# State space chunks begun ahead of the preceding chunk's state, convolution steps spread over the projections, queries projected ahead of gates

## The reference, cut to what matters

```python
# layer of the first network (conv branch): 31 taps, depthwise, 256 wide
u = conv_in * sigmoid(conv_gate)
y = conv_b + sum(u_padded[:, k:k+T] * conv_w[k] for k in range(31))
y = silu(layernorm(y) * ln_g + ln_b) * silu(out_gate)
# differential attention: k, q rotated; two softmaxes of 48-wide heads, subtracted,
# normed, times silu(gate)

def rwkv7_step(S, inp):
    r_t, w_t, k_t, v_t, kk_t, a_t = inp
    sa = jnp.einsum("bhvk,bhk->bhv", S, -kk_t)
    S = (S * w_t[:, :, None, :]
         + jnp.einsum("bhv,bhk->bhvk", sa, kk_t * a_t)
         + jnp.einsum("bhv,bhk->bhvk", v_t, k_t))
    y = jnp.einsum("bhvk,bhk->bhv", S, r_t)
    return S, y
```

## Time and profile before

| | us |
|---|---|
| median of 3 runs | 3750.78 |
| lowest, highest | 3741.96, 3754.45 |
| the profiled execution | 3754.05 |
| its span in the trace | 3752.3 |
| TensorE busy in the span | 3362.2 (90%) |
| late stage of layer 0, projections to first scores | about 285 to 513 |
| late stage of layer 1, same | about 900 to 1064 |
| chunks of the matrix recurrence | about 1818 to 2154 |

### The profile page before, as it was taken

How to read it: one execution, slowest core, us unless ns; L and a number is a source line. 1 busy time by engine, 2 the same in 40 slices (tenths; PEclk the granted TensorE clock), 3 DMA queues, 4 the chain that set the end, 5 groups by cost and what they waited for, 6 DMA issues and landing times.

```text
span 3752.3 us, 40013 instructions
## 1 busy us (share of the span) xinstructions
PE 3362.2 (90%) x16212; PEld 2633.0 (70%) x16212; DVE 1673.2 (45%) x2537; ACT 1226.9 (33%) x2071; POOL 737.2 (20%) x547
## 2 busy tenths in 40 slices
PE   3999687799988999986699889999999999989998
PEld 1878565587766788864577757887788876567886
DVE  2153556324864634353533345343634342445344
ACT  2242155334254322322221233223322233733222
POOL 1203111431413100163211130000100053240000
PEclk6999898899998999998776789999999999999999
DMA  4303110121102232322000012323232321012322
GB/s 182 109 36 113 68 37 15 56 90 43 61 11 75 80 98 97 96 76 72 1 1 1 1 51 85 101 91 100 79 96 99 93 89 62 1 51 93 104 92 77
DMA packets 77575, 260.95 MB, mean 70 GB/s; under 512 B 8400, under 2 KB 9552, under 8 KB 76240
## 3 DMA queue, kind: packets, MB, share of 16 engines
q1 hardware_dynamic: 76528, 253.67, 20.5%
q0 software_dynamic: 864, 4.72, 0.4%
HBM read 256.26 MB, written 2.10 MB: 69 GB/s over the span
## 4 chain that ended last, share of the span: by engine, by line
PE 82%; DVE 10%; ACT 4%; POOL 2%; issue 1%; DMA 1%; SPq 0%; POOLq 0%; ACTq 0%; DVEq 0%
PE banks L343 81%; DVE area L1659 2%; PE banks L352 1%; DMA x_lat<-in_xt 1%; POOL area L400 1%; DVE area L852 1%; DVE area L551 1%; DVE small L1713 1%; POOL w_lo L334 1%; DVE x_lat L554 0%; DVE area L472 0%; DVE area L2459 0%; DVE area L461 0%; ACT area L417 0%; ACT w_hi L324 0%
## 5 line engine op out<-in xcount | busy, mean ns | idle before, releaser
L343 PE MATMUL banks<-area,w_hi 128*128 128x512 f32 (+4 forms) x5896 | 1777.9, 385 | 60.6 <-POOL w_lo L334 27.1
L343 PEld LDWEIGHTS banks<-area,w_hi 128*128 128x128 f32 (+2 forms) x5896 | 1085.9, 189 | 324.5 <-issue 52.6
L343 PE MATMUL banks<-area,w_lo 128*128 128x512 f32 (+3 forms) x2948 | 1125.3, 383 | 0.0
L343 PE MATMUL banks<-area,area 128*128 128x64 f32 (+11 forms) x3888 | 590.1, 356 | 73.6 <-DVE area L2503 12.1
L343 PEld LDWEIGHTS banks<-area,w_lo 128*128 128x128 f32 (+2 forms) x2948 | 558.5, 189 | 119.6
L343 PE MATMUL banks<-area,w_late 128*128 128x512 f32 (+2 forms) x2316 | 576.4, 398 | 39.3 <-ACT area L507 21.1
L343 PEld LDWEIGHTS banks<-area,area 128*128 128x128 f32 (+4 forms) x3888 | 464.4, 203 | 194.7 <-issue 101.1
L343 PEld LDWEIGHTS banks<-area,w_late 128*128 128x128 f32 (+1 forms) x2316 | 435.0, 190 | 153.6 <-ACT area L507 24.4
L324 ACT ACTIVATE w_hi<-w_raw 128x1024 fp32r<-128x1024 f32 (+2 forms) x361 | 349.5, 971 | 560.5 <-PE banks L343 432.4
L400 POOL TENSOR_TENSOR area<-area,area 128x512 f32<-128x512 f32 (+1 forms) x114 | 152.5, 1340 | 1536.8 <-ACT area L385 1534.2
L334 POOL TENSOR_TENSOR w_lo<-w_raw,w_hi 128x1024 fp32r<-128x1024 f32 (+1 forms) x133 | 302.9, 2280 | 512.2 <-ACT w_hi L324 512.2
(11 more groups left out here) (235 smaller groups left out, 2329.4 us busy)
## 6 DMA issues: line engine op xcount, KB each, us to landing
w_raw<-in_l_ffn_w_in SPq DMA_DIRECT2D x176, 512.0 KB, 3.3
w_raw<-in_l_ffn_w_out SPq DMA_DIRECT2D x128, 384.0 KB, 3.1
w_raw<-in_w_in SPq DMA_DIRECT2D x66, 512.0 KB, 3.5
w_raw<-in_w_mod SPq DMA_DIRECT2D x32, 512.0 KB, 5.0
w_raw<-in_w_qkv SPq DMA_DIRECT2D x24, 512.0 KB, 3.3
w_raw<-in_l_w_in SPq DMA_DIRECT2D x22, 512.0 KB, 3.3
w_raw<-in_w_out SPq DMA_DIRECT2D x32, 320.0 KB, 2.9
area<-in_w_mod SPq DMA_DIRECT2D x8, 1024.0 KB, 14.2
```

Source lines behind the costliest of these rows:

```text
L343: return e.matmul(out, lhsT, rhs, start=first, stop=stop, skip_group_check=True)
```

## The change

In `LateStage` the queries are projected ahead of the gates, on all engines and in the order of the weights, and the layer norm's steps move to the groups of the gates. The 62 taps are dealt out by a table: 10 after the convolution's inputs (ahead of modulation third 1), 6 behind it, then 4 per rotation of the keys, 2 (layer 0) or 4 (layer 1) per copy of the values, then the copy of modulation third 2, then 4 or 2 per rotation of the queries, and the rest. In `EvenMixer` a chunk is cut into begin (masked B, xs), keys (tok, masked K), levels and state; begin of chunk c+1 is issued between levels and state of chunk c, and keys of c+1 after the state part of c. For this `xt_m` and `m_rb_t` have two buffers, in space from a smaller `levels` table (8 masks instead of 14) and from two dead tiles.

```diff
-LATE_GROUPS = (8, 9, 2, 3, 7, 6)
+LATE_GROUPS = (8, 9, 2, 3, 6, 7)
 class LateStage:
-            TAPS_EACH = 4
-                self.ln_at = {"mean": 1, "sum": (4, 6), "square": (2, 5), "root": (5, 7)} if two else {
-                    "mean": 0, "sum": (2,), "square": (1,), "root": (3,)}
+                self.taps_at = (10, 6, 4, 2, 4) if two else (10, 6, 4, 4, 2)
+                self.ln_at = {"mean": 1, "square": (1, 3), "sum": (2, 4), "root": (2, 4), "silu": 6} if two else {
+                    "mean": 0, "square": (0,), "sum": (1,), "root": (1,), "silu": 2}
 # pe
                 self.mod_pe(q, e, 2)
-                self.g_of.pe(q, e)
                 self.rope_pe(q, e, self.q_of, "q")
+                gates = [(m, s) for m, s, *_ in self.g_of.each()]
+                self.g_of.pe(q, e, lambda q, e, m, s: self.ln_pe(q, e, gates.index((m, s))))
                 self.mod_pe(q, e, 3)
 # dve
                 self.conv_dve(q, e)
+                taps = self.taps(q, e)
+                for _ in range(self.taps_at[0]):
+                    next(taps, None)
                 self.mod_dve(q, e, 1)
-                self.rope_dve(q, e, self.k_of, "k", some_taps)
-                self.v_of.dve(q, e, some_taps)
+                for _ in range(self.taps_at[1]):
+                    next(taps, None)
+                some = lambda n: lambda i: [next(taps, None) for _ in range(n)]
+                self.rope_dve(q, e, self.k_of, "k", some(self.taps_at[2]))
+                self.v_of.dve(q, e, some(self.taps_at[3]))
+                self.mod_dve(q, e, 2)
+                self.rope_dve(q, e, self.q_of, "q", some(self.taps_at[4]))
                 for _ in taps:
                     pass
-                self.mod_dve(q, e, 2)
-                self.rope_dve(q, e, self.q_of, "q", lambda i: self.ln_dve(q, e, i))
+                self.ln_dve(q, e)
                 self.mod_dve(q, e, 3)
 class EvenMixer:
 # pe
+                self.begin_pe(q, e, 0)
+                self.keys_pe(q, e, 0)
                 for c in range(NCH):
-                    self.chunk_pe(q, e, c, beside)
+                    self.levels_pe(q, e, c, beside)
+                    if c + 1 < NCH:
+                        self.begin_pe(q, e, c + 1)
+                    self.state_pe(q, e, c, beside)
+                    if c + 1 < NCH:
+                        self.keys_pe(q, e, c + 1)
 # dve
+                    self.levels_dve(q, e, c, beside)
+                    self.mid_dve(q, e, c)
+                    next(beside, None)
+                    if c + 1 < NCH:
+                        self.begin_dve(q, e, c + 1)
+                    self.state_dve(q, e, c)
+                    if c + 1 < NCH:
+                        self.keys_dve(q, e, c + 1)
+            def begin_dve(self, q, e, c):
                 if c:
-                    q.wait_ge(*at(self.tag, "made", "y", c - 1))
+                    for g in range(2):
+                        q.wait_ge(*at(self.tag, "off", c - 1, 6, g))
+                        q.wait_ge(*at(self.tag, "made", "t1", c - 1, 6, g))
+                if c >= 2:
+                    q.wait_ge(*at(self.tag, "made", "y", c - 2))
...
+            def keys_dve(self, q, e, c):
+                if c:
+                    q.wait_ge(*at(self.tag, "made", "y", c - 1))
+                for half in range(2):
+                    self.masked_dve(q, e, c, "K", half)
```

More of the change, by code:

```diff
@@ L1447, in rope_act @@
                         q.wait_ge(*at("turned", t))
-                for g, (m, s, c0, c1, u, bank) in enumerate(project.each()):
+                for m, s, c0, c1, u, bank in project.each():
                     round_weights(q, e, project.pieces[m])
@@ L1601, in act @@
                 self.v_of.act(q, e)
-                for m, s, c0, c1, u, bank in self.g_of.each():
+                self.rope_act(q, e, self.q_of, "q", self.qd)
+                for g, (m, s, c0, c1, u, bank) in enumerate(self.g_of.each()):
                     round_weights(q, e, self.g_of.pieces[m])
@@ L1958, in __init__ @@
                 self.tot = place.take(4, 3 * NCH)
-                self.levels = place.take(14, P)
+                self.levels = place.take(8, P)
                 chunk_at = place.at
@@ L2008, in __init__, with books_masked @@
                     self.books("var heads", p), self.books("gate", p)
+            def books_masked(self, c, kind):
+                if kind == "K":
+                    for i in range(3):
+                        self.books("tok", c, i)
+                for half in range(2):
+                    for odd in range(2):
+                        self.books("masked", c, kind, half, odd)
+                if kind == "B":
+                    for g in range(2):
+                        self.books("xs", c, g)
             def books(self, *key):
@@ L2125, in masked_pe, with begin_pe @@
                     self.made(t, *key)
-            def chunk_pe(self, q, e, c, beside):
+            def begin_pe(self, q, e, c):
                 cs = slice(c * CH, (c + 1) * CH)
-                if c == 0:
-                    for who in ("dve", "act", "pool"):
-                        q.wait_ge(*at("fence", who, "even chunks"))
-                for i in range(3):
-                    src, dst = self.tok(i, c)
-                    self.bank_free(q, "tok", c, i)
-                    for p in range(4):
-                        t = turned(e, self.bank("tok", c, i)[:, p * P:(p + 1) * P], src(p))
-                    self.made(t, "tok", c, i)
                 for half in range(2):
@@ L2146, in chunk_pe, with keys_pe, levels_pe @@
                     self.made(t, "xs", c, g)
+            def keys_pe(self, q, e, c):
+                for i in range(3):
+                    src, dst = self.tok(i, c)
+                    self.bank_free(q, "tok", c, i)
+                    for p in range(4):
+                        t = turned(e, self.bank("tok", c, i)[:, p * P:(p + 1) * P], src(p))
+                    self.made(t, "tok", c, i)
                 for half in range(2):
                     self.masked_pe(q, e, c, "K", self.k_t, half)
+            def levels_pe(self, q, e, c, beside):
                 for n_l in range(1, 7):
```

125 lines of the change are left out of this document (66 added, 59 removed).

## The result

The changed kernel takes 3659.34 us, the median of four runs (3654.36 to 3670.15), against 3750.59 us for the kernel before (3741.96 to 3754.45): a ratio of 0.9764, with a 95% interval of 0.9735 to 0.9793. The forecast was 3652, the range 3630 to 3690.

A forecast was written before the change was run, and what follows sets the result against it. TensorE was taken as the bound (82% of the chain of waits), through its waits and half clock. Terms 31.6 + 12.2 + 14.5 + 13.5 + 27.4 = 99.2 us off 3754.05, less 3.3 for the median, gave 3652 us; range 3630 to 3690.

The forecast's parts named there:

- Layer 0: Late stage of layer 0: 33.4 us wait for VectorE's rows' copy becomes 5.6, stage end gains 4.8, 1.0 lost: 31.6 us gained.
- "I take 0" for the ten taps ahead of third 1: Layer 0: taps moved into VectorE's silences were taken to cost nothing; without that cover the price is 3 us.
- A wait for L334 over 2 us: Sign that the forecast is wrong: TensorE newly waiting over 2 us for L334, a low half of weights from GpSimd.
- Layer 1: Late stage of layer 1: 3.6 us tap wait goes, half clock returns 2.5, the end gains about 6.1: 12.2 us.
- Chunks, idle time: Chunks: inverse wait gone in three of four (9.1 us), scaled-state wait filled (net 3.6), chunk 0 earlier (1.8): 14.5 us.
- Chunks, clock of the levels: Chunks, ahead of the levels: no wait after y, so 11.2 us at half clock become full, three times: 13.5 us.
- Chunks, clock of the state part: Chunks, rhs to y: two of three state parts taken at full clock, 27.4 us; 0 and 41 kept as ends.
- the first rival: State part of the chunks: three small waits keep its clock from ever holding, term 0; 3679 us, chance 0.30.
- the fourth: Late stages: GpSimd, slowed beside taps, starves TensorE of weights, kernel slower; 3769 us, chance 0.03 together with a null result.
- the second: Chunks: even the levels stay at half clock for their first 13 us, only idle time goes; 3693 us, chance 0.06.
- third: Chunks: all three state parts hold full clock and the levels' waits shrink too; 3638 us or less, chance 0.13.
- fifth: Layer 0: TensorE still stands at modulation third 2 for another reason, layer 0 gives only 4; 3680 us, chance 0.03.

## Why the prediction was right, and where it was not

The time is 7 us above the forecast, inside the range. That it is so near is in part luck: the largest term in doubt, 27.4 us, came to nothing, and some 16 us that the working did not have (behind layer 1, in the levels and in the waits of the chunks) made up for more than half of it. Step by step, on the profiled execution (83.9 us against 99.2):

- **Layer 0, 31.6 us: 27.1 measured.** The wait went from 33.4 to 6.8 us where 5.6 was worked out, 26.6 us instead of 27.8. The end of the stage and all the rest, by difference, gave 4.5, where the working had 3.8 (4.8 less 1.0). Two terms were not in it: 2.4 us for the low half, and 1.6 us by which this execution was already late ahead of the stage (VectorE's last product there at 304.18, before at 302.60). "I take 0" for the ten taps ahead of third 1 was the step that failed: I had asked what VectorE's silence covers and not what GpSimd does in it. A wait for L334 over 2 us was among the signs of being wrong, and it came, at one place.
- **Layer 1, 12.2 us: 12.5 measured** (39.6 less 27.1). The tap wait is gone, and ahead of the scores 0.94 us are left. (The working took 0.2 us off for what stays there, though it named 0.7.)
- **Behind layer 1** lie 6.8 us that I had not counted (46.4 less 39.6). The run with the late stages alone has 7.1 us there too (50.5 less 43.4), so it comes with that half of the change; which part of it is attention at another clock no run tells.
- **Chunks, idle time, 14.5 us: 16.7 measured** (20.8 less 1.8 and 2.3). The wait of about 0.95 us for a bank ahead of rhs did not come: rhs takes the banks of the first masked products, and VectorE had read these by 1825.39 (L2531), just as TensorE came to rhs. By the busy times of the two traces the idle time fell from 29.3 to 12.8 us, which agrees.
- **Chunks, clock of the levels, 13.5 us: some 20.8, by difference** (37.5 less 16.7). The return just behind y came as foretold. The rest of these 20.8 us is not the first half of the levels alone. In chunks 0 to 2 rhs now runs longer at 2.4 GHz before the clock falls: it took some 7.3 us instead of 8.67 in chunk 0 and some 6.4 instead of 9.93 in chunk 2. Against that, y of chunk 3 took 13.35 us where it had taken 8.43.
- **Chunks, clock of the state part, 27.4 us: next to nothing** (what rhs won, some 5 us in all, y of chunk 3 lost again). This is the step that failed, and the first rival's outcome for this term (that rival's time, 3679 us, did not come, since the other terms of the chunks gave more). I had asked whether the small waits would lose the clock. In the changed kernel they were not the cause: it fell ahead of all of them, in a stretch without a wait, and with full fillers it passed the same waits at 2.4 GHz in 10 of 12 state parts. In the other two it fell right behind them (for 3 us in one, through y in the other), so the question was not an empty one. The bound of 41 us for three state parts was right in kind: y took 7.59 us instead of the 6.4 that I had worked out, sa 2.23 instead of 2.3, turns 1.53 instead of 1.45.

The rule of the page "TensorE: Matmul & The Clock Gate", section "A second HAM failure mode: psum-queue depth-cycling", of the Trainium skill gives this term as 0 as well, through short idles between groups. The outcome agrees, the reason does not: in chunk 0 of the changed kernel no idle stood in the 20 us ahead of the fall, and the idles of 0.56 us stayed in the runs that kept the clock. For the two falls right behind such idles the rule is not ruled out.

Of the rivals, the fourth (GpSimd starves TensorE) was real as a mechanism and small in price, 2.4 us at one place of some 60; the second, third and fifth did not occur.

What stays open: why the same chunk code gets the clock back at other moments from one kernel to the next. In the traces of the changed kernel and of the one with the taps moved, the same stretch from the turns of chunk 0 to those of chunk 3 takes 221.0 and 213.0 us, and one wait of 2.16 us in the levels loses the clock in some traces and not in others. So what fillers do to a single chunk is not certain in advance; that they carry the clock through rhs and sa held in 12 of 12. Nor was any size between 128 and 256 columns tried, or other data in the fillers. And whether a real product, not an unread one, can be given 128 rows at this place was not tried.

## What to carry to other kernels

A TensorE that is busy all the time can still be at half its clock. So look at the granted clock window by window, and at the shape of the products where it falls, before a wait is blamed. Where small products on part of the array follow each other, work on all 128 rows between them can more than pay for itself (3631.6 against 3649.11 us). Test the size: with 128 columns, or on 64 rows, the fillers here gave nothing back.

When VectorE's work is moved into a silence of its own, ask what GpSimd does in that silence. Two low halves took 8.32 us there instead of about 4.8 (twice 2.39), and putting six of the ten steps elsewhere brought them back to 2.39 each.

## What the runs showed of the hardware that I had not expected

- The clock fell from 2.4 to 1.2 GHz in a stretch of 14 us without any idle time of TensorE (1816 to 1830), in the block of rhs products with 64 columns, and stayed down for 22 us in which TensorE was busy for 21.16.
- Eight unread products of 256 columns per chunk on 128 rows kept it at 2.4 GHz through rhs and sa wherever rhs began at 2.4 GHz (3656.65 us, sa 2.23 instead of 4.05 us); the same on 64 rows did not (3682.42 us), and neither did 128 columns on 128 rows (3673.51 us).
- Behind such fillers the two small waits (0.56 and 0.43 us) left it at 2.4 GHz in 10 of 12 state parts. One of 2.33 us ahead of rhs ended it. One of 2.16 us in the levels of chunk 0 ended it in the changed kernel and not in the run with steps moved and fillers.
